# Gate of the small experts in two passes, and gathered rows copied as high and low parts, in a two-layer decoder trunk

## The reference, cut to what matters

```python
def swiglu(xn, w_gate, w_up, w_down):
    return (jax.nn.silu(xn @ w_gate) * (xn @ w_up)) @ w_down

def moe_swiglu(xn, w_router, w_gate, w_up, w_down):
    top_v, top_i = lax.top_k((xn @ w_router), TOP_K)            # 2 of 8 experts per token
    top_w = jax.nn.softmax(top_v, axis=-1)
    gates = jnp.sum(jax.nn.one_hot(top_i, N_EXPERTS) * top_w[..., None], axis=-2)
    for e in range(N_EXPERTS):                                   # D_FF_EXPERT = 3584
        out = out + gates[..., e:e + 1] * swiglu(xn, w_gate[e], w_up[e], w_down[e])
```

## Time and profile before

| what | value |
|---|---|
| median of 3 runs | 1334.09 us |
| the profiled execution's own time | 1336.44 us |
| its span in the profile | 1334.7 us |
| TensorE (PE) matmuls | 1310.8 us, 98% |
| TensorE weight loads | 1092.7 us, 82% |
| VectorE (DVE) | 1148.5 us, 86% |
| ScalarE (ACT) | 948.0 us, 71% |
| read from HBM | 420.27 MB |
| chain that ended last | PE 88%, DVE 7%, ACT 2%, issue 2%, DMA 1% |

### The profile page before, as it was taken

How to read it: one execution, slowest core, us unless ns; L and a number is a source line. 1 busy time by engine, 2 the same in 40 slices (tenths; PEclk the granted TensorE clock), 3 DMA queues, 4 the chain that set the end, 5 groups by cost and what they waited for, 6 DMA issues and landing times.

```text
span 1334.7 us, 17325 instructions
## 1 busy us (share of the span) xinstructions
PE 1310.8 (98%) x6404; PEld 1092.7 (82%) x6404; DVE 1148.5 (86%) x963; ACT 948.0 (71%) x879; POOL 72.4 (5%) x133
## 2 busy tenths in 40 slices
PE   8999999999998999999999999999999999999998
PEld 7876888888887888888888788888888888888887
DVE  6896765556888989999999999999999999999886
ACT  5676644445775777778887778777777777777765
POOL 2120830000200000000000000000000000000000
PEclk9999999999999999999999999999999999999999
DMA  9733765555368999999999999999999999999970
GB/s 309 257 128 90 253 201 191 189 192 172 127 256 319 350 327 353 397 397 397 399 398 399 395 378 398 397 397 397 397 379 384 398 399 399 393 398 390 364 265 32
DMA packets 183524, 422.46 MB, mean 317 GB/s; under 512 B 13064, under 2 KB 37392, under 8 KB 169104
## 3 DMA queue, kind: packets, MB, share of 16 engines
q1 hardware_dynamic: 183440, 421.35, 85.6%
HBM read 420.27 MB, written 1.05 MB: 316 GB/s over the span
## 4 chain that ended last, share of the span: by engine, by line
PE 88%; DVE 7%; ACT 2%; issue 2%; DMA 1%; SPq 0%; POOL 0%; DVEq 0%; ACTq 0%; POOLq 0%
PE ps L363 21%; PE ps L365 21%; PE ps L364 21%; PE ps L977 5%; PE ps L1136 5%; PE ps L1137 5%; PE ps L975 3%; DVE w_lo L342 3%; PE ps L954 1%; PE ps L1117 1%; PE ps L957 1%; PE ps L1130 1%; ACT w_hi L324 1%; PE ps L974 1%; DMA raw<-in_attn_w_qkv_dram 1%
## 5 line engine op out<-in xcount | busy, mean ns | idle before, releaser
L342 DVE TENSOR_TENSOR w_lo<-raw,w_hi 128x2048 fp32r<-128x2048 f32 x308 | 701.7, 2290 | 86.1 <-ACT w_hi L324 85.2
L324 ACT ACTIVATE w_hi<-raw 128x2048 fp32r<-128x2048 f32 x311 | 591.6, 1917 | 150.9 <-PE ps L365 143.6
L342 DVE TENSOR_TENSOR w_more<-raw,w_more 128x2048 fp32r<-128x2048 f32 x74 | 169.4, 2289 | 14.8 <-ACT w_more L324 14.6
L324 ACT ACTIVATE w_more<-raw 128x2048 fp32r<-128x2048 f32 x74 | 142.0, 1919 | 40.5 <-PE ps L365 38.6
L363 PE MATMUL ps<-w_hi,h_t_hi 128*128 128x512 f32 x348 | 136.3, 392 | 1.6 <-DVE w_lo L342 1.6
L365 PE MATMUL ps<-w_hi,h_t_lo 128*128 128x512 f32 x348 | 135.5, 389 | 0.0
L364 PE MATMUL ps<-w_lo,h_t_hi 128*128 128x512 f32 x348 | 135.5, 389 | 0.0
L363 PE MATMUL ps<-w_hi,xe 128*128 128x512 f32 x284 | 112.4, 396 | 1.6 <-DVE w_lo L342 1.5
L365 PE MATMUL ps<-w_hi,xe 128*128 128x512 f32 x284 | 111.4, 392 | 0.0
L364 PE MATMUL ps<-w_lo,xe 128*128 128x512 f32 x284 | 111.3, 392 | 0.0
L977 PE MATMUL ps<-a_all,w_hi 128*128 128x512 f32 x308 | 109.8, 396 | 0.0
(11 more groups left out here) (357 smaller groups left out, 2311.6 us busy)
## 6 DMA issues: line engine op xcount, KB each, us to landing
raw<-in_moe_w_gate_dram SPq DMA_DIRECT2D x112, 1024.0 KB, 9.2
raw<-in_moe_w_up_dram SPq DMA_DIRECT2D x111, 1024.0 KB, 9.4
raw<-in_moe_w_down_dram SPq DMA_DIRECT2D x111, 1024.0 KB, 9.5
raw<-in_attn_w_qkv_dram SPq DMA_DIRECT2D x11, 1024.0 KB, 12.9
raw<-in_ffn_w_gate_dram SPq DMA_DIRECT2D x11, 1024.0 KB, 5.4
raw<-in_ffn_w_up_dram SPq DMA_DIRECT2D x11, 1024.0 KB, 5.3
raw<-in_ffn_w_down_dram SPq DMA_DIRECT2D x11, 1024.0 KB, 5.0
raw<-in_ple_w_gate_dram SPq DMA_DIRECT2D x8, 1024.0 KB, 5.5
```

What stands on the lines that cost most here:

```text
L324: nc.scalar.activation(hi, raw_slot(u), ACT.Copy).then_inc(hi_ready, 1)
L342: nc.vector.tensor_tensor(lo, raw_slot(u), hi.bitcast(F32), ALU.subtract).then_inc(lo_ready, 1)
```

## The change

For the small expert, gate is now done in two passes like up. Its two halves must be added before Silu, so ScalarE copies gate and up as they stand (`copy_few_gate`, `copy_few_up`), TensorE folds both into bank 2 (`fold_few`, 8 folds instead of 4), one unit earlier than the old place; ScalarE applies Silu to the folded 128x256 (`silus_few`), VectorE multiplies (`hiddens_few`), and the product, now in SBUF, is split (`few_hi`, `few_lo`). `few_lo` stands at step n = 3 of the large block, the old low part at n = 2.

In the gather, a chunk's high and low rows no longer add up but go to the two halves of a bank, and ScalarE copies both at once for each expert (`copy_chunk`). A chunk fills a bank, and the chunks go round banks 5, 2 and 0. VectorE has no part in it. The chunks' places are 1 after the first up unit, 2 after the second, 3 after the first down unit and 2 after the second.

```diff
-        PIECE_BANKS = (5, 2, 5, 2)
+        CHUNK_BANKS = (5, 2, 0, 5, 2, 0, 5, 2)
+        CHUNKS_AFTER = {2: (0,), 3: (1, 2), 4: (3, 4, 5), 5: (6, 7)}
...
+            def fold_few(g, k=0):
+                pe.wait_ge(silu_ready, g + 1 + FB * k)
+                pe.wait_ge(hidden_ready, g + 1 + FB * k)
+                pe.wait_ge(ht_lo_ready, g + FB * k)
+                for at, of in ((0, silu), (4 * FEW, hidden)):
+                    for n in range(4):
+                        last = nc.tensor.matmul(ps[:, 2, at + n * FEW:at + (n + 1) * FEW], turned_columns(of, n), fold[:, :],
                                                 start=True, stop=True)
...
+            def gather_chunk(c, k, g):
+                if c == 1:
+                    pe.wait_ge(ht_lo_ready, g)
+                if c == 2:
+                    pe.wait_ge(silu_ready, g + 1)
+                if c > 2:
+                    pe.wait_ge(x_copied, c - 2 + 4 * k)
+                for h, rows in enumerate((a_hi, a_lo)):
+                    for tt in range(TT):
+                        last = nc.tensor.matmul(ps[:, CHUNK_BANKS[c], h * 2 * SLOTS:(h + 1) * 2 * SLOTS], ...
...
-                    if few and n == 1:
+                    if few:
                         both = x[:, 2 * d * P + FEW:2 * d * P + FEW + P]
                         last = product_few(ps[:, n, :], both, w, d == 0, d == KD - 1)
...
+                            if n == 0 and half == 0 and e:
+                                fold_few(g - 1, k)
...
+            def copy_few_gate(g, u, k):
+                used(u, k)
+                act.wait_ge(hidden_ready, g + FB * k)
+                nc.scalar.activation(silu, ps[:, 0, :], ACT.Copy).then_inc(silu_ready, 1)
+            def copy_few_up(g, u, k):
+                used(u, k)
+                act.wait_ge(hidden_transposed, g - JF + FB * k)
+                nc.scalar.activation(hidden, ps[:, 1, :], ACT.Copy).then_inc(hidden_ready, 1)
+            def silus_few(g, f, k):
+                act.wait_ge(hidden_transposed, g - JF + 1 + FB * k)
+                nc.scalar.activation(few_silu, ps[:, 2, 0:4 * FEW], ACT.Silu).then_inc(few_silu_ready, 2)
+            def few_hi(f, k):
+                act.wait_ge(few_product_ready, 2 * f + 2 + FB * k)
...
+            def copy_chunk(c, k):
+                act.wait_ge(gathered, 3 + c + 4 * k)
                 for e, x in enumerate((xe_parts, xb_parts)):
+                    last = nc.scalar.activation(x[:, c, :, :], gathered_of(c, e), ACT.Copy)
+                last.then_inc(x_copied, 1)
...
-                        if n == 2:
-                            hidden_lo(g - 1, k, few=e == 1)
-                        if n == (3 if bare else 4):
+                        if n == 1 and e:
+                            hiddens_few(f, k)
+                        if n == 3 and e:
+                            few_lo(g - 1, k)
+                        if n == 2 and not e:
+                            hidden_lo(g - 1, k)
+                        if n == 4 and e:
                             hiddens(g, u + 3, k)
```

More of the change, by code:

```diff
@@ L952, in transpose_hidden @@
                 for n in range(4):
-                    if few:
-                        last = nc.tensor.matmul(ps[:, 2, n * FEW:(n + 1) * FEW], hidden_rows(n), fold[:, :],
+                    last = nc.tensor.transpose(ps[:, 2, n * P:(n + 1) * P], turned_columns(hidden, n), ident[:, :])
+                last.then_inc(hidden_transposed, 1)
+            def fold_few(g, k=0):
[5 more added lines that the diff above has]
+                        last = nc.tensor.matmul(ps[:, 2, at + n * FEW:at + (n + 1) * FEW], turned_columns(of, n), fold[:, :],
                                                 start=True, stop=True)
-                        continue
-                    last = nc.tensor.transpose(ps[:, 2, n * P:(n + 1) * P], hidden_rows(n), ident[:, :])
                 last.then_inc(hidden_transposed, 1)
@@ L1109, in gather_piece @@
                         pe.wait_ge(rows_split_lo, 2)
[L1110 to L1116, removed]
-                        last = nc.tensor.matmul(ps[:, PIECE_BANKS[i], cols:cols + 2 * SLOTS],
+                if c == 1:
[6 more added lines that the diff above has]
+                    for tt in range(TT):
+                        last = nc.tensor.matmul(ps[:, CHUNK_BANKS[c], h * 2 * SLOTS:(h + 1) * 2 * SLOTS],
                                                 rows[:, tt * D + c * P:tt * D + (c + 1) * P],
                                                 pick[:, tt * 2 * SLOTS:(tt + 1) * 2 * SLOTS],
-                                                start=rows is a_hi and tt == 0, stop=rows is a_lo and tt == 1)
+                                                start=tt == 0, stop=tt == 1)
                 last.then_inc(gathered, 1)
@@ L1190, in first_turn @@
                             if gather and n:
-                                gather_piece(half, 0, g)
+                                for c in CHUNKS_AFTER[2 + half]:
+                                    gather_chunk(c, 0, g)
                         if f == 1 and n == 0:
@@ L1200, in first_turn @@
                         if gather:
-                            gather_piece(2, 0, g)
-                            gather_piece(3, 0, g)
+                            for c in CHUNKS_AFTER[4]:
+                                gather_chunk(c, 0, g)
                         down(u + 5, f - 1, 1, g - 1, 0)
-                        if not gather:
+                        if gather:
+                            for c in CHUNKS_AFTER[5]:
+                                gather_chunk(c, 0, g)
+                        else:
                             transpose_hidden(g)
@@ L1231, in pair @@
                             if f == FB - 1 and e == 1 and n == 1:
-                                gather_piece(half, k + 2, g + FB * k)
+                                for c in CHUNKS_AFTER[2 + half]:
+                                    gather_chunk(c, k + 2, g + FB * k)
                             between(2 * n + half)
@@ L1242, in pair @@
                     if f == FB - 1 and e == 1:
[L1243 to L1244 removed]
+                        for c in CHUNKS_AFTER[4]:
+                            gather_chunk(c, k + 2, g + FB * k)
                     down(u + 5, f_down, 1, g_down, t_down, k, few=few)
+                    if f == FB - 1 and e == 1:
+                        for c in CHUNKS_AFTER[5]:
+                            gather_chunk(c, k + 2, g + FB * k)
                     between(5)
@@ L1707, in pair @@
                             result_hi(u - 1, 0, k, free=not first)
-                        if n == 2:
-                            hidden_hi(g - 1, k, few=e == 1)
+                        if n == 1 and e:
+                            silus_few(g - 1, f, k)
+                        if n == 2 and e:
+                            few_hi(f, k)
                             silus(g, u + 1, k)
+                        if n == 2 and not e:
+                            hidden_hi(g - 1, k)
+                            copy_few_gate(g, u + 1, k)
+                        if n == (3 if first and f == 0 else 4) and not e:
+                            copy_few_up(g, u + 3, k)
                         if f == 3 and e == 0 and n == 3:
```

103 lines of the change are left out of this document (36 added, 67 removed).

## The result

The changed kernel takes 1340.93 us (median of 7 runs, 1339.29 to 1342.08), the kernel before on the same chip 1335.08 us (7 runs, 1333.81 to 1337.07). The ratio is 1.0039, 95% interval 1.0029 to 1.0048: slower by some 5.2 us (by the ratio) where -0.4 was forecast, and 1.9 us above the range of 1328 to 1339. The profiled execution took 1342.08 us, the longest of the seven, with a span of 1340.3 us.

The account below looks back on a forecast made before the run. Transfers at 399 GB/s were taken to bound the pairs (31.5 us a double block, TensorE 29.6). Recovered rate -2.5, first gather +0.7 and last gather +1.4 gave -0.4 on 1334.09: 1333.7 us, range 1328 to 1339.

Parts of the forecast that it names:

- Chunk 1's wait: In later gathers, chunk 1 waits for the small low part, ready 4.7 us after ScalarE starts the next turn's first unit.
- last end: Last gather: from ScalarE's start on the last turn's first unit to TensorE's matmul, 13.4 us instead of 11.8; costs 1.4 us.
- y_lo waits: At two pair starts TensorE waits 3.0 us in all for VectorE's y_lo; 2.7 us less VectorE gather work ends this.
- recovered transfers: At the pairs' starts transfers run below 399 GB/s, losing 5.0 us; half, 2.5 us, was taken as regained.
- The step that failed: Inside pairs, clock falls behind TensorE's waits hide behind the transfers, with 1.9 us of room a block.
- first gather: ScalarE must copy chunks 6 and 7 before its next split, so loads come 0.7 us late for good.
- Rival 3: TensorE's waits lower its clock, each fall near the last gather costing 1.7 us: 1336 to 1340 us; chance 0.2.
- The copies of a gather: Per gather, all 16 copies go to ScalarE: about +2.2 us for ScalarE and -2.7 us for VectorE.
- TensorE alone: Two-pass gate saves 18.2 us net and ended y_lo waits 3.0: about 21 us if TensorE alone counted.
- I cost both at nothing: Small block: ScalarE's extra work of about 1 us and VectorE's 0.26 us relief were charged as zero.
- Rival 1: Pair stage: 399 GB/s is only what was asked for, so TensorE's 21 us show: 1313 us; chance 0.07.

Follow-up runs that it names:

- e1: Changed kernel, but after the first gather chunk 1 waits for the small product instead of its low part: 1331.83 us, ratio 0.9976 to the kernel before.
- e8: The best version: e1 with ScalarE's next split ahead of the copies of chunks 6 and 7 in the first gather: 1330.32 us, ratio 0.9961.
- e12: Changed kernel with the old gather put back, its piece 1 waiting for the small product instead of the low part: 1331.32 us, ratio 0.9971.
- e2: Changed kernel with the small low part back at step n = 2, chunk 1 still waiting for it: 1331.75 us, ratio 0.9974.
- e3: Changed kernel with the old gather put back, keeping the two-pass gate and the late low part: 1335.08 us, ratio 0.9997 to the kernel before.
- e4: Kernel before with only the new gather in chunks, three-pass gate, low part at its old step: 1338.13 us, ratio 1.0017.
- e7: Kernel before with only the small block's low part one step later in VectorE's queue (n = 3 instead of 2): 1339.65 us, ratio 1.0036.

## Why the prediction failed, point by point

**Right.** Once the wait is out, the transfers pace the pairs (397 to 399 GB/s in e1, and 5.3 us for half loads in the best version), and the queue is full until a pair's end. Chunk 1's wait stands where it was worked out: ScalarE's start to TensorE's chunk 1 is 4.6 us at the first pair's end (710.32 to 714.94) and at the last (1160.36 to 1164.98), against the 4.7 forecast, and the last end is 13.49 us against 13.4, up from 11.77. The y_lo waits went. The two 50-us stretches at the starts of the pairs rise to 397 and 398 GB/s once the wait is out (e1), and the *rest* of e1, e8 and e12, -2.8 to -3.4 us, is near the -2.5 taken for recovered transfers. That nearness is in part luck: the kernel before has a fall of the clock in its stage (at 965) that these have not, and at an equal mean clock e1 and e2 gain 1.5 to 2 us in all.

**The step that failed** is "In the middle of a pair such falls hide behind the transfers, with 1.9 us of room a block". The sum charged the late low part at the last gather alone, and at the inner pair ends put it at nothing. At the two inner pair ends it delays TensorE by 2.5 us of wait, and the clock adds 1.6. These 4.1 us are more than the slots' reserve: splits, then slots, then loads come late, and what the transfers lose there they don't make up. Measured: 4.9 us at two ends. e3 shows that the step would have been right for a delay of 2 us. Added up from the terms in the table, the change is +1.8 (first gather) +1.7 (last end) +1.4 (rest) = +4.9 us, where the forecast had +0.7, +1.4 and -2.5.

**Rival 3** had the mechanism and the sign. It put the falls of the clock near the last gather and wanted two of them there; they came behind the two inner gathers (0.66 at 715 and at 940), and none at the last (1.00 at 1165). Its 1336 to 1340 was the nearest of the rivals, still 0.9 us short. I weighed the rule of the Trainium skill's page "TensorE: Matmul & The Clock Gate", section "Part 1: The HAM clock gate (the "warmup" mystery)", that the slow clock is what an engine falls back to when it is kept waiting: the two falls agree with it, and the wait at the last gather, the longest, does not show it.

**Terms that were mis-sized.** The copies of a gather, +2.2 and -2.7 us, are not 8 times the 380 and 419 ns of the earlier trace rows, which is 3.0 and 3.4, but 8 distances of two starts (0.27 and 0.33 us); the sum does not hang on it. *First gather:* +0.7 forecast, 1.8 measured (6.41 against 4.61). I set TensorE's 0.94 us of chunks against it, but ScalarE first waits for these chunks too (0.98 us, to 504.54), and then their four copies stand before the split. *TensorE alone:* 21 us forecast, 11.3 measured. "I cost both at nothing" was wrong for VectorE, whose splits alone take 2.2 us a unit against TensorE's 1.81 in a small block; with gate at three passes two of six units had covered for it. The weight loads' waits for the split, 8.8 us against 0.7, are most of the 9.7 us that are missing. It had no effect on the result, since the transfers allow less than that anyway. *y_lo:* the waits ended, but not by the 2.7 us that the gather takes off VectorE (e4 keeps 3.1 us of them); the gate did it, and by which of its moves was not tried.

**Rival 1** is out. The slices of the pair stage never pass 400 GB/s in any kernel, and the half loads give 5.3 us to the best version. The 21 us of this rival do not come with half loads either. The Trainium skill's page "DMA: Bandwidth & Descriptors", section "Where 436 GB/s comes from", has 435 GB/s as the ports' limit; no run here came near it over a slice.

**Open.** Why the clock falls behind one wait and not behind another. How the 4.9 us of the two inner ends divide between wait and clock: no profile has a wait of 2.5 us there without the fall. An estimate from the executions at a mean clock of 0.997: the changed kernel is 5 us above e1 and e2, and the last end explains 2.7 of it (13.49 against 10.77), so some 2.3 us at the inner ends would be the wait's own and the rest the clock's. Where the clock fell in these executions, no trace shows.

## What to carry to other kernels

When a step is moved behind an instruction that waits for a transfer, it inherits that transfer's landing, and so does everyone who waits for the step: search for each semaphore that the moved step raises, and wait for the last reader of the buffer (here the product) rather than for a later step that happened to imply it. Where two resources stand within a few per cent, price such a stall at every place where it occurs, not only at the last one: here a delay of 2 us at an inner pair end was free, and one of 4 us cost 2.4 us for good. Compare single executions at an equal mean clock before a difference of a few us is put down to the change alone. And bound a saving on one engine by the pace of the engine that feeds it, block by block and not on the mean.

## What the hardware showed that was not expected

The length of a TensorE wait does not say whether the clock falls behind it. It fell behind waits of 1.56 us (before, to 0.66), 1.45 and 1.65 (e4), 2.49 and 2.61 (after), and stayed at 1.00 behind 1.44 (before), 2.05 (e3) and 2.99 us (after). The same two waits for y_lo, 1.44 and 1.56 us, have the fall behind the second in the kernel before and behind the first in e7. Each of the two falls of the changed kernel took 1.6 us (5.38 against 3.79 for the same work). And a fuller queue brought no higher rate: the transfers moved 401 GB/s with a median of 8.0 us from issue to landing (before, gate units, 520 to 560), and 398 with 13.5 us (after, 650 to 700). Nor does this time by itself tell the rate: at 765 to 800, in the dip of both kernels, it is 7.8 to 8.6 us, and the rate is 378 GB/s.
